# Pooling projection of chunks 0 and 1 on rows that have only the modulation's scale, with the decode tile moved to chunk 2 and the pooling matrix folded into w_out

## The reference, cut to what matters

```python
mod = silu(c) @ w_ada + b_ada          # -> sh1, sc1, gt1, sh2, sc2, gt2, 1024 each
h = rmsnorm(x, g_pre_mix) * (1 + sc1) + sh1
v_pool, x_conv, gate_b, gate_c = split(h @ w_in)        # 512 columns each
# pooling: 4 groups of 128 channels, trailing windows of 2, 4, 8, 16 rows
d = mean_window(v_pool) - v_pool       # the first rows divide by the rows there are
y_pool = (d @ pool_w[group]) * pool_scale
conv_in = gate_c * x_conv
y_conv = gate_b * causal_dwconv3(conv_in)
x = x + gt1 * rmsnorm(concat(y_pool, y_conv) @ w_out, g_post_mix)
h2 = rmsnorm(x, g_pre_ffn) * (1 + sc2) + sh2
u = causal_dwconv3(h2 @ ffn_w_up); a, b = split(u)
x = x + gt2 * rmsnorm((silu(a) * b) @ ffn_w_down, g_post_ffn)
```

## Time and profile before

| | |
|---|---|
| median of 3 runs | 779.73 us (759.44 to 779.76) |
| the profiled execution | 758.07 us, span 756.4 us on its slowest core |
| TensorE busy | 92% of the span |
| VectorE, ScalarE, GpSimd busy | 65%, 46%, 28% |
| chain that ended last | TensorE 75%, loads 11%, VectorE 5% |
| span of the 8 cores | 749.1 to 756.4 us |

### The profile page before, as it was taken

The page is one execution under the profiler, slowest core; times in us unless marked ns, Lnnn a source line. Parts: engine busy times, 40 slices in busy tenths (PEclk is TensorE's granted clock), DMA queues, the critical chain, the costliest instruction groups (busy, mean ns, idle before and its releaser), DMA issues.

```text
span 756.4 us, 11992 instructions; the slowest of 8 cores (749.1 to 756.4 us)
## 1 busy us (share of the span) xinstructions
PE 693.2 (92%) x4032; PEld 333.1 (44%) x4032; DVE 491.1 (65%) x645; ACT 350.0 (46%) x621; POOL 213.1 (28%) x259
## 2 busy tenths in 40 slices
PE   0169889989999999999999999999999999999996
PEld 0134444444544444444444444444444444444443
DVE  0247857777886888996777522248888888833222
ACT  1325825563647787666454321125454454531111
POOL 4101200011100332235544400005667667540000
PEclk9979999999999999999999999999999999999999
DMA  8999995299624798559997422334443434013311
GB/s 152 206 188 243 204 206 99 86 225 166 177 103 151 173 213 185 140 136 186 170 163 133 77 83 112 113 112 88 81 84 58 82 67 76 2 42 125 112 70 56
DMA packets 30552, 97.28 MB, mean 129 GB/s; under 512 B 4480, under 2 KB 4992, under 8 KB 30364
## 3 DMA queue, kind: packets, MB, share of 16 engines
q0 software_dynamic: 17088, 54.06, 41.5%
q1 hardware_dynamic: 13404, 42.47, 16.6%
HBM read 125.28 MB, written 19.07 MB: 191 GB/s over the span
## 4 chain that ended last, share of the span: by engine, by line
PE 75%; DMA 11%; DVE 5%; issue 4%; ACT 3%; POOL 1%; DVEq 0%; ACTq 0%; POOLq 0%
PE ps L797 46%; PE ps L298 21%; PE ps L289 6%; DMA arena<-w_ada 6%; DMA arena<-w_in_p 5%; DVE arena L1190 2%; POOL arena L543 1%; ACT arena L562 1%; ACT arena L716 1%; PE ps L306 1%; DVE arena L763 1%; DVE arena L953 1%; DVE arena L957 0%; DVE arena L1194 0%; ACT arena L1188 0%
## 5 line engine op out<-in xcount | busy, mean ns | idle before, releaser
L797 PE MATMUL ps<-arena 128*128 128x512 bf16 (+1 forms) x2400 | 440.2, 344 | 9.5 <-DMA arena<-w_in_p 5.2
L797 PEld LDWEIGHTS ps<-arena 128*128 128x128 bf16 x2400 | 201.8, 98 | 237.8 <-issue 19.1
L298 PE MATMUL ps<-arena 128*128 128x512 bf16 (+1 forms) x748 | 161.9, 379 | 0.0
L1190 DVE SCALAR_TENSOR_TENSOR arena<-ps,arena 128x1023 f32<-128x1023 f32 x88 | 112.6, 1280 | 39.8 <-ACT arena L1188 39.8
L1204 POOL TENSOR_TENSOR arena<-arena 128x1024 bf16<-128x1024 f32 x44 | 104.0, 2364 | 97.9 <-DVE arena L1194 59.3
L1194 DVE SCALAR_TENSOR_TENSOR arena<-ps,arena 128x1022 f32<-128x1022 f32 x88 | 112.8, 1282 | 9.1
L298 PEld LDWEIGHTS ps<-arena 128*128 128x128 bf16 (+1 forms) x748 | 73.7, 99 | 87.9 <-issue 0.4
L569 DVE RECIPROCAL arena<-arena 128x1 f32<-128x1 f32 (+1 forms) x67 | 10.7, 159 | 139.1 <-ACT arena L564 138.6
L1188 ACT ACTIVATE arena<-ps,arena 128x1024 f32<-128x1024 f32 x88 | 97.6, 1109 | 0.1
L562 ACT ACTIVATE arena<-ps 128x1024 f32<-128x1024 f32 (+1 forms) x33 | 33.7, 1022 | 137.2 <-PE ps L298 119.4
L289 PE MATMUL ps<-arena 128*128 128x512 bf16 (+2 forms) x352 | 76.2, 363 | 4.6 <-DMA arena<-w_ada 3.3
(11 more groups left out here) (89 smaller groups left out, 379.8 us busy)
## 6 DMA issues: line engine op xcount, KB each, us to landing
arena<-w_up POOLq DMA_DIRECT2D x44, 512.0 KB, 6.0
y<-arena SPq DMA_DIRECT2D x32, 512.0 KB, 2.7
arena<-w_ada POOLq DMA_DIRECT2D x24, 512.0 KB, 15.5
arena<-x SPq DMA_DIRECT2D x22, 512.0 KB, 8.2
arena<-y SPq DMA_DIRECT2D x16, 512.0 KB, 3.4
arena<-w_down POOLq DMA_DIRECT2D x11, 512.0 KB, 11.0
arena<-x POOLq DMA_DIRECT2D x10, 512.0 KB, 22.1
arena<-w_in_j POOLq DMA_DIRECT2D x4, 768.0 KB, 39.7
```

The lines of the kernel that those rows point to most:

```text
L298: inst = e.matmul(out_ap, lhs_list[i], rhs_list[i], start=(first and i == 0), stop=(last and i == n - 1))
L797: inst = e.matmul(o_, l_, r_, start=st, stop=sp_)
L1190: K.op("dve", lambda e: e.scalar_tensor_tensor(tv[:, 1:1024], psv[:, 0:1023], fw_of(1, c), tv[:, 1:1024], ALU.mult, ALU.add), reads=rp + [ ...
```

## The change

The shift of the modulation adds a constant per channel to all rows of the prompt. The pooling takes the mean of a window minus the row, for the first rows as well, so that constant cancels. The change uses this for chunks 0 and 1:

- It loads the scale's weights, `w_in_p` and x tiles 4 to 7 first, and the shift's weights after them. The transposed rows are evicted with the scale alone (`h_ev0`) into `HB[0]` and `HB[1]`, and all eight pooling projections (`P_mm`) of chunks 0 and 1 run on these.
- When the shift is there, chunk 0's transposed rows, which are still in their banks, are evicted once more with scale and shift; chunk 1's are transposed again. The windows (`P_win`) write directly to `BY`.
- Then come the eight `V_item`s of chunks 0 and 1, with the decode columns in chunk 1, in the order (0,0) (1,0) (0,1) (1,1) (0,2) (0,3) (1,2) (1,3), the windows of chunk 1 behind the first four.
- The decode tile's pooling projection goes with chunk 2. Chunk 2's history needs the shift: the last 16 rows of chunk 1 are put behind the decode columns in `HS` and projected along with them.
- `PW_item` and `PWS_item` are gone. The pooling matrix, scaled by `pool_scale`, is multiplied into the first four blocks of `w_out` once (`wfold`: 8 wide matmuls, four evictions).
- The gates come as a block behind the `V_item`s, the load of `VS` behind them, then the fold, then the loop from n = 8 on. For tiles 8 to 15 the row scaling is on ScalarE.

```diff
 def h_dve(t):
+        if 8 <= t < 16:
+            K.op("act", lambda e: e.activation(out=xn[0:rows, :], in_=XT[xi][0:rows, :], func=AF.Copy, scale=STAT[0:rows, ST_RS1, t:t + 1]),
+                 reads=[r_xt[xi], r_stat[ST_RS1][t]], writes=[r_xn])
+        else:
...
+    pada_load(1)
     dma1("pool", flat(WINP), winp_d, writes=[r_win[0]])
-    dma1("pool", flat(POOLW), pw_d, writes=[r_poolw])
-    winj_load(0)
...
-    h_load(16)
-    h_act(16)
-    h_dve(16)
-    winj_load(1)
-    h_load(4, "pool")
-    h_load(5, "pool")
-    winj_load(2)
-    h_load(6, "pool")
-    h_load(7, "pool")
-    winj_load(3)
-    dma1("pool", VS.rearrange("p a b c -> p (a b c)"), stp_d, writes=r_vs)
+    for t in range(4, 8):
+        h_load(t, "pool")
+    pada_load(0)
+    winj_load(0)
+    dma1("pool", PWF, pw_d, writes=[r_pwf])
+    for j in range(1, 4):
+        winj_load(j)
     dma1("pool", QS.rearrange("p a b c -> p (a b c)"), stc_d, writes=r_qs)
...
+    def h_ev0(gi, bank, eng, dst, r_dst):
+                if eng == "act":
+                    inst = e.activation(out=o_, in_=i_, func=AF.Copy, scale=G1T[:, kc, 0:1])
+                else:
+                    inst = e.tensor_scalar(o_, i_, G1T[:, kc, 0:1], None, ALU.mult)
...
-    misc_set = [[6, 7, 1]]
+    misc_set = [[6, 7, 0, 1]]
...
-        BP = 0 if p_n[0] <= 6 and p_n[0] % 2 == 0 else 5
+        BP = 2 if p_n[0] <= 8 and p_n[0] % 2 == 0 else 5
...
+        if samp:
+            K.op("act", lambda e: e.activation(out=V[:, 0:16], in_=PS[:, sbank, TS:TS + 16], func=AF.Copy), reads=[r_ps[sbank]], writes=[rV])
...
-        Dt, rD = DB[g % 2], r_db[g % 2]
+        Dt, rD = BY[c % 3][:, g, :], r_by[c][g]
...
+    def wfold(g):
+        b = 0 if g % 2 == 0 else 6
+        for hb in range(2):
+            op = K.op("pe", mm_group(PS[:, b + hb, :], [POOLW[:, g, :]], [WOUT[:, g, hb * 512:(hb + 1) * 512]]),
+                      reads=[r_poolw, r_wout[0]], writes=[r_ps[b + hb]])
+        K.op("act", lambda e: e.activation(out=WOUT[:, g, :], in_=PS[:, b:b + 2, :].rearrange("p a n -> p (a n)"), func=AF.Copy),
+             reads=[r_ps[b], r_ps[b + 1]], writes=[r_wfold[g]])
...
+    for gi in range(4):
+        h_tr(gi, raw_banks[gi], XN1, r_xn1)
+    for p in range(4):
+        ada_piece(1, p, 4 + p % 2, G1T, r_g1, 0, V_GPRE)
+    for gi in range(4):
+        h_ev0(gi, raw_banks[gi], ("act", "dve")[gi % 2], HB[0], r_hb[0][gi])
+    for g in range(4):
+        P_mm(0, g, False)
+    for t in range(4, 8):
+        h_act(t)
+        h_dve(t)
+    for gi in range(4):
+        h_tr(gi, 3 + gi % 2, XN1, r_xn1)
+        h_ev0(gi, 3 + gi % 2, "act", HB[1], r_hb[1][gi])
+    h_load(16)
+    h_act(16)
+    h_dve(16)
+    for p in range(4):
+        ada_piece(0, p, 3 + p % 2, S1T, r_s1, V_BADA, None)
+    for g in range(4):
+        P_win(0, g, False, None)
+        P_mm(1, g, False)
+    for gi in range(4):
+        h_ev(gi, raw_banks[gi], ("act", "dve")[gi % 2], G1T, S1T, [r_g1, r_s1], HB[0], 0, r_hb[0][gi])
+    for gi in range(4):
+        h_T(1, gi, misc_bank(), ("act", "dve")[gi % 2])
+    samp_tr_ev(misc_bank(), XN2[0], r_xn2[0], G1T, S1T, [r_g1, r_s1], HS, 0, r_hs)
+    K.op("act", lambda e: e.activation(out=HS[:, :, TS:TS + 16], in_=HB[1][:, :, 496:512], func=AF.Copy), reads=r_hb[1], writes=[r_hs])
...
+    for t in range(8, 12):
+        h_load(t, "pool")
...
+    wout_load()
+    for p in range(2):
+        ada_load(2, p)
+    for k, (c, j) in enumerate(((0, 0), (1, 0), (0, 1), (1, 1), (0, 2), (0, 3), (1, 2), (1, 3))):
+        if k == 6:
+            for gi in range(4):
+                h_T(2, gi, misc_bank(), "act" if gi < 3 else "dve")
+        V_item(c, j, c == 1)
+        if k < 4:
+            P_win(1, k, False, None)
+        if k in (2, 3):
+            for t in (8, 9) if k == 2 else (10, 11):
+                h_act(t)
+                h_dve(t)
+    for p in range(4):
+        gate_piece(2, p, misc_bank(), ROWB1, ROWG1, r_rows1, GT1P, GT1S, r_gt1)
+        if p < 2:
+            ada_load(2, p + 2)
+        else:
+            ada_load(4, p - 2)
+        if p == 1:
+            for t in (12, 13):
+                h_load(t, "pool")
+    dma1("pool", VS.rearrange("p a b c -> p (a b c)"), stp_d, writes=r_vs)
+    for g in range(4):
+        wfold(g)
+    misc_set[0] = [6, 7]
     LAG = 8
-    for n in range(16):
+    for n in range(8, 16):
         c, s = n // 4, n % 4
-        samp = (c == 1)
+        samp = (c == 2)
...
-        P_item(c, s, samp)
-        V_item(c, s, samp)
-        if n >= 1:
-            PW_item((n - 1) // 4, (n - 1) % 4)
-        if n == 9:
-            PWS_item()
+        last_p = P_item(c, s, samp)
+        V_item(c, s, False)
```

More of the change, by code:

```diff
@@ L422, in build_program @@
     ACC = alloc([128, 512], F32)
-    DB = [alloc([128, 512], BF16) for _ in range(2)]
     VS = alloc([128, 4, NS, PB + DS], F32)
@@ L799, in mm_seq @@
         return f
-    for rr in r_wout + [r for c in range(2) for r in r_by[c]]:
-        rr.alias(r_pada)
     def wout_load():
@@ new lines, in build_program @@
+    for rr in [r for c in range(2) for r in r_by[c]]:
+        rr.alias(r_pada[4:8])
+    wout_load()
[12 more added lines that the diff above has]
+                h_dve(t)
```

139 lines of the change are left out of this document (55 added, 84 removed).

## The result

The changed kernel takes 770.12 us (median of 6 runs, 769.66 to 773.62) against 761.69 for the kernel before on the same chip: ratio 1.0144, 95% interval 1.0126 to 1.0161; the two medians by themselves stand 1.1% apart. So it is 1.1 to 1.4% slower, which is within the 2% called the same, but it lies outside the predicted 742 to 768, and it went up where the forecast went down. The profiled execution took 770.08 us, with a span of 768.5 on core 2.

What follows compares the result with a forecast made beforehand. The prediction took TensorE as the bound, busy 693.2 of 756.4 us. The first w_out matmul 4.0 us earlier and -0.6 behind it made -4.6, so 758.1 becomes 753.5; range 742 to 768.

Steps and rivals of the forecast that it cites:

- Step 1: Loads at the start: the first w_in_j, which the gated-convolution projection needs, lands at 60.0 us, where before it landed at 52.0.
- Step 2: Work ahead of the convolution: both chunks' scale-only projections fit before the loads end; convolution starts at 61.5 us.
- the upper end of 65: Latest convolution start allowed in Step 2, 65 us, if VectorE and ScalarE get in each other's way.
- the mark: Start of the first w_out matmul: 127.53 us before, predicted at 123.5, 4.0 earlier.
- Step 3: Convolution start to the mark: 54.6 us TensorE work, 2.4 low clock, 5 waits; the gate weights' 3.3 us wait goes.
- Step 4: Behind the mark: pooling matmuls removed, decode columns of the pooling projection added; net -0.6 us.
- the prediction's own sign: Check on Step 4: the distance from the mark to the end stays within 2 us of before.
- C: Rival: pool state's load, queued behind late gates, holds ScalarE in chunk 2's first item; 14 us lost, 767.5; chance 0.15.
- B: Rival: chunk 1's 32 moved matmuls run at half clock, 6.9 us more; start at 65.4, end at 757.4; chance 0.13.
- A: Rival: loads alone bound the stretch to the mark, which comes at 116.6, 10.9 earlier; time 743.6; chance 0.17.

Runs made afterwards that it cites:

- kernel 4: The changed kernel with the scale's four pieces put ahead of the reciprocals and scaling of x tiles 2 and 3: ratio 1.0070 to the kernel before.
- kernel 1: The changed kernel itself, unaltered, run again on another chip (its second run): ratio 1.0073 to the kernel before.
- Kernel 5: kernel 4 plus the decode tile's square behind chunk 1's first evictions and the squares of tiles 4 to 6 ahead of the first projection's evictions: 763.76 us, ratio 0.9950.
- kernel 10: Kernel 5 with two gate pieces earlier, and chunk 1 projected on modulated rows between the convolution items (half the change undone): 767.29 us, ratio 1.0041.
- kernel 8: Kernel 5 with two gate pieces earlier, chunk 1's evictions split over ScalarE and VectorE, and 24 useless matmuls keeping TensorE busy: 762.85 us, ratio 0.9969.
- kernel 9: kernel 8 with the squares of x tiles 8 to 11 held behind the second convolution item's product: ratio 0.9906; a version without the useless matmuls and split evictions: 765.47 us.

## Why the prediction was wrong, by its steps

**Step 1 was right within 2 us.** The first `w_in_j` was predicted for 60.0 and landed at 40.3 + 21.8 = 62.1; the shift's pieces landed from 46.7 to 57.6. That "no engine of the DMA runs dry" did not hold: tile 7's load and the shift's issues behind it came at 37.60 and later, and from 36.5 to 40.5 the DMA engines were busy 8% of the time. By the price that the prediction itself put on this it costs 2 us. Issued near 40 on GpSimd's queue:

```profile
arena<-w_in_j POOLq DMA_DIRECT2D x1, 768.0 KB, 21.8
arena<-w_ada POOLq DMA_DIRECT2D x1, 512.0 KB, 17.7
```

**Step 2 failed: 61.5 predicted, 80.70 measured, 19.2 late.** It counted what VectorE has to do between 41.5 and 60, 18.5 us, and took the rest as hidden. VectorE did have time to spare; what set the start was a chain through three engines, and the prediction left four of its links out.
- "one eviction later, near 39, the scale-only projection starts": it came at 45.29. The transposes were 2.6 later than in the earlier trace rows, and the scale pieces came behind them. With the pieces ahead it comes at 41.6 instead of 44.8 (medians of the cores, kernels 4 and 1), so 3.2 of the 6.3 us were theirs.
- ScalarE's work was not added up (it is named only for the upper end of 65): the squares of tiles 4 to 7 and the projection's evictions in turns, and chunk 1's eight scale-only evictions, 4.91 us on ScalarE alone.
- "The decode tile's load waits on SP for a freed slot, with nothing behind it before the mark": on SP's queue that is true (the next issue there is at 103.65). But the square that reads the tile stands in ScalarE's order, and behind it those eight evictions: 5.71 us.
- Both bursts ran partly at the low clock (granted at 0.83 and 0.88 on average): 8.23 and 7.74 us here against 6.91 in the earlier trace rows.

Kernel 5, which mends the first and third of these and part of the second, brings the start from 81.7 to 71.1 and the time down by 8.5: the late start is the cause, shown. The rest of the way to the loads' 62, 4 us in kernel 10 and 7 to 9 in the others of the ordered ones, was won by no kernel here.

**Step 3** allowed too much where it looked and missed what came behind. From 80.70 to 127.5 TensorE is idle for 0.8 us and at full clock, where 2.4 for the clock and 5 for waits were allowed. The gate weights' wait, said to go, is there as in the earlier trace rows, in the line at 137.69:

```profile
137.69 2.41 PE L289 MATMUL ps<-arena 128*18 128x256 bf16 x9 [3.15 <-DMA arena<-w_ada]
139.88 3.62 PE L801 MATMUL ps<-arena 128*128 128x512 bf16 x8
```

The block of gates ran behind the last item; the second pair's weights were asked for at 128.71, and after the wait 8 wide matmuls took 3.62 us at a clock of 0.50, where 1.89 is usual. The mark itself was a poor yardstick: work of chunk 2 slid ahead of it, and the first w_out matmul came at 152.75, not 123.5.

**The sum from the start on was right, its split is not shown.** From the first convolution item to the end of the span the prediction has 753.5 - 1.7 - 61.5 = 690.3 us, the trace 768.5 - 80.70 = 687.8. So the whole miss of 16.6 us is, to 0.1, the 19.2 of step 2 less 2.5. In part that is luck: from 80.70 to 152.75 TensorE is idle for 4.2 us and loses 1.7 to the clock behind the gates, near the 7.4 that step 3 allowed, but in another place. Step 4 by itself can't be read, since the mark moved against the work: from it to the end it is 615.8 us, 628.9 before, and by the prediction's own sign (within 2 us) that is a miss.

**The rivals.** C, slower than before, came nearest in time (767.5), but for another reason: its gates did run late, as it said, and cost 3.15 us and the clock behind; its wait for the pool state did not come (that load landed at 153.3, and no wait of ScalarE for it is in the trace). The eight cores say more of these gates: the three on which TensorE did not wait for their weights (0, 3 and 4) end at 760.6 to 762.2 us, the five on which it did (1.0 to 3.2 us) at 766.8 to 768.5. That they go together is shown; that the wait is the cause is not, for with the gates early the cores still spread from 759.8 to 767.1. B priced the low clock at 6.9 us for chunk 1; the bursts lost 2.2 us together here and 4.8 in the second run (of these, 2.5 in a burst for which the rows give a clock of 1.00). B's own sign, a clock under 0.8 from 39 to 61, was not met: it was 0.86, and 0.71 from 60 to 80.7. The Trainium skill ("TensorE: Matmul & The Clock Gate", section "HAM oscillation — how this bites in real kernels") says that bursts between waits for loads begin at the low clock each time. The trace agrees in part: the 8 wide matmuls behind the gates' wait for their weights ran at 0.50, and the two bursts, behind waits for evictions, at 0.83 and 0.88; but the 32 transposes behind a wait of 21.9 us took 3.57 us, 1.95 for 32 others at 77.76, and for both the rows give a clock of 1.00. What the clock was worth at the start kernel 8 shows: kept up, it moved the start by 2.7 us and the median span by about 2, not 6.9. A, the loads alone, was not reached: kernels 8 and 9 show that an earlier start meets the next load, x tile 8 and then the gate weights.

## What to carry to other kernels

Before work is moved ahead of a load, write down the chain that must run there link by link, through every engine's queue in order, and not the busy time of the engine that looks fullest: here three engines were 70% busy and the chain was the bound. Whatever waits for a load in an in-order queue has the whole queue behind it, so ask where the instruction stands that reads the load, not only where the load is issued. And when a start is made earlier, look up what comes next on every queue before counting the gain: of the 10.6 us that kernel 5 won at the start 8.5 reached the time, of the 8.2 that kernel 4 won nothing did, and behind it, on four cores, a store on SP's queue and the load that stands behind it came late. Last, compare small gains over all runs of all cores: by one profiled execution kernel 8 had gained nothing, by all of them 2 us.

## What the runs showed of the hardware

The decode tile's 256 KB on SP's queue took 9.1 us while GpSimd's queue was full; of the traffic in that time SP's queue had the smaller part. Issue at 52.33, and the two queues from 52.9 to 61.45 us (packets, MB, time as a share of 16 engines):

```profile
arena<-x SPq DMA_DIRECT2D x1, 256.0 KB, 9.1
...
q0 software_dynamic: 300, 1.35, 90.4%
q1 hardware_dynamic: 80, 0.26, 11.2%
```

So a small load on the second queue was not quick here: the median of the 22 loads of twice its size on that queue was 5.0 us in this run. That the eight cores of one run, with the same program, differ by 12 us (755.0 to 766.9 in kernel 4) was not expected either. The slowest sets the time: there the median core gained 4.7 us of span on the changed kernel, the time nothing (772.29 to 772.52).
